# Splitting the branch and gate products of block 1 into quarters of the contraction, between seven parts of the modulation weights

## The reference

```
mod = silu(c) @ w_ada + b_ada                  # w_ada: 2048 x 6144
shift, scale, gate = split(mod, 3)
h = rms_norm(x) * (1 + scale) + shift
xr, gr, qc, kvc, kr, ga = split(h @ w_in)      # widths 1024, 1024, 512, 512, 64, 1024
y_rnn = rg_lru(conv4(xr)) * silu(gr)           # causal conv of width 4, two 64x64 block gates, scan
y_att = mla(rms(qc) @ w_uq, rms(kvc) @ w_ukv, rope(kr)) * silu(ga)    # 8 heads, causal
x = x + gate * (concat(y_rnn, y_att) @ w_out)
```

## Time and profile before

| what | us |
|---|---|
| median of 3 runs (lowest, highest) | 2844.11 (2840.98, 2847.81) |
| the profiled execution's own time | 2841.78 |
| its span, first to last instruction | 2840.0 |
| TensorE busy in the span | 2769.7 (98%) |
| first lora product starts | 56.62 |
| last lora product ends | 201.03 |
| output product of block 1 starts | about 415 |

### The profile page before, as it was taken

The page is one execution under the profiler, slowest core; times in us unless marked ns, Lnnn a source line. Parts: engine busy times, 40 slices in busy tenths (PEclk is TensorE's granted clock), DMA queues, the critical chain, the costliest instruction groups (busy, mean ns, idle before and its releaser), DMA issues.

```text
span 2840.0 us, 43925 instructions
## 1 busy us (share of the span) xinstructions
PE 2769.7 (98%) x15316; PEld 2382.7 (84%) x15316; DVE 1964.4 (69%) x2557; ACT 1191.3 (42%) x1519; POOL 5.7 (0%) x10
## 2 busy tenths in 40 slices
PE   5999999999999999999999999999999999999999
PEld 3778788888878888888888888888888888888888
DVE  5446457666766777756777775687777775677765
ACT  1012434444444444444444443355444444444443
POOL 0000000000000000000000000000000000000000
PEclk9999999999999999999999999999999999999999
DMA  9787556544444666656666566654466666666664
GB/s 328 249 267 210 192 171 193 167 137 156 148 134 155 187 190 185 185 190 187 191 185 186 181 198 190 185 163 128 150 188 183 188 188 191 186 189 185 190 197 146
DMA packets 693729, 526.63 MB, mean 185 GB/s; under 512 B 28877, under 2 KB 674831, under 8 KB 693391
## 3 DMA queue, kind: packets, MB, share of 16 engines
q1 hardware_dynamic: 690448, 521.04, 59.8%
q10 hardware_dynamic: 3199, 4.48, 0.4%
HBM read 523.34 MB, written 2.10 MB: 185 GB/s over the span
## 4 chain that ended last, share of the span: by engine, by line
PE 91%; DVE 4%; issue 2%; ACT 2%; DMA 1%; ACTq 0%; DVEq 0%; SPq 0%
PE acc L623 76%; PE acc L704 3%; PE acc L882 2%; PE acc L688 1%; PE turned L704 1%; DVE wr L1622 1%; PE sums L704 1%; DVE pro_ada L1697 1%; PE mixed L804 1%; PE sums L999 1%; PE sums L631 0%; PE mixed L1004 0%; DMA pro_xrow<-in_x 0%; ACTq L1212 0%; ACT wr L1181 0%
## 5 line engine op out<-in xcount | busy, mean ns | idle before, releaser
L623 PE MATMUL acc<-xs,wr 128*128 128x512 f32 (+1 forms) x7680 | 1365.2, 339 | 1.1 <-DVE wr L1622 1.1
L623 PEld LDWEIGHTS acc<-xs,wr 128*128 128x128 f32 x7680 | 1176.6, 188 | 177.4 <-issue 7.2
L1622 DVE TENSOR_TENSOR wr<-raw,wr 128x1024 fp32r<-128x1024 f32 x832 | 1001.3, 1222 | 360.4 <-ACT wr L1181 348.7
L1181 ACT ACTIVATE wr<-raw 128x1024 fp32r<-128x1024 f32 x832 | 869.6, 1056 | 816.6 <-PE acc L623 809.2
L623 PE MATMUL acc<-ys,wr 128*128 128x512 f32 (+1 forms) x4352 | 770.0, 339 | 6.0 <-DVE ys L1656 5.8
L623 PEld LDWEIGHTS acc<-ys,wr 128*128 128x128 f32 x4352 | 668.8, 189 | 102.6 <-DVE ys L1656 6.4
L623 PE MATMUL acc<-wr,xs 128*128 128x512 f32 (+1 forms) x1024 | 190.1, 344 | 0.0
L623 PEld LDWEIGHTS acc<-wr,xs 128*128 128x128 f32 x1024 | 158.2, 188 | 27.0 <-issue 4.3
L1515 ACT ACTIVATE ffn_cv<-ffn_cv 128x256 f32<-128x256 f32 x88 | 36.8, 419 | 245.5 <-DVE ffn_cv L2177 245.5
L1633 DVE TENSOR_REDUCE ffn_ug<-acc 128x512 f32<-128x1024 f32 x88 | 107.7, 1224 | 42.6 <-PE acc L623 42.6
L1697 DVE SCALAR_TENSOR_TENSOR pro_ada<-aring,small,pro_ada 128x1024 f32<-128x1024 f32 (+1 forms) x80 | 85.6, 1070 | 59.5 <-DMA aring<-in_w_ada 55.3
(11 more groups left out here) (297 smaller groups left out, 1492.2 us busy)
## 6 DMA issues: line engine op xcount, KB each, us to landing
raw<-in_ffn_w_up SPq DMA_DIRECT2D x704, 256.0 KB
raw<-in_ffn_w_down SPq DMA_DIRECT2D x160, 512.0 KB
raw<-in_a_w_qkv SPq DMA_DIRECT2D x96, 512.0 KB
raw<-in_b_w_kv SPq DMA_DIRECT2D x64, 512.0 KB
aring<-in_w_ada SPq DMA_DIRECT2D x48, 512.0 KB, 10.6
w<-in_w_in SPq DMA_DIRECT2D x48, 512.0 KB
raw<-in_w_ada SPq DMA_DIRECT2D x32, 512.0 KB, 5.1
raw<-in_w_out SPq DMA_DIRECT2D x32, 512.0 KB
```

The source lines that it names most:

```text
L623: mm = pe.matmul(*ops, start=first and ops is wide, stop=last and ops is wide)
L1181: f(wr[:, s, :, 0:256], raw[:, s, :].rearrange("p (k n) -> p k n", k=UK), ACT.Copy)\
L1622: tt(wr[:, s, :, 256:512], raw[:, s, :].rearrange("p (k n) -> p k n", k=UK), wr[:, s, :, 0:256], ALU.subtract).then_inc(T.unit_split[s].se ...
```

## The change

- `ADA_PARTS` has seven parts in place of five: tiles 0-1, 2-3, 4-5, 6-7, 8-11, 12-13, 14-15. A load for a part of two tiles is 256 KB in runs of 1 KB; for four tiles 512 KB in runs of 2 KB.
- xr and gr are made in quarters of the contraction. Quarter 0 of all 8 pairs is put aside by ScalarE; quarters 1 and 2 are added to `half` by VectorE (`quarter_out`). Quarter 3 comes after the loras for xr and after U_PAIRS for gr.
- TensorE's order: parts 0 and 1 with lora(0..3); quarter 0, then part 2; lora(4), lora(5), part 3, lora(6), lora(7); quarter 1, then part 4; lora(8..11); quarter 2 with part 5 in it; lora(12), part 6, lora(13..15). SyncE's loads are reordered to match.
- The ring holds variable spans of one area of 8192 columns (1152 for lora, 1024 for the rest).
- The 64 columns of kr are loaded twice, side by side, and multiplied in one matmul of 128 columns.
- x is loaded by SyncE ahead of w_ada, not by ScalarE after the vectors. Its transposes come before those of the vectors and use two PSUM banks in turn.
- The roots' sums of q, kv and kr each stand behind their own unit of xr.
- ScalarE evaluates the recurrence's gates g-1 before it waits for v unit g, not after.
- gr's last quarter stands before ga, with the attention heads starting in it. The recurrent half of the output is gated within the head loop, ahead of the attention half, and the output product takes the contraction tiles from 0 instead of from 8.

```diff
-ADA_PARTS = [(0, 4), (4, 4), (8, 4), (12, 2), (14, 2)]
+ADA_PARTS = [(0, 2), (2, 2), (4, 2), (6, 2), (8, 4), (12, 2), (14, 2)]
-LORA_COLS = 2 * LORA + ROPE
+LORA_COLS = 2 * LORA + 2 * ROPE
+ONE_RING, ONE_SPACE = 8, RING * UK * 512
...
+            sp.dma_start(xrow[:, :, :], t["x"][0]...)          # SyncE, before the positions
...
+            for part in range(2):
+                for r in range(KT):
+                    ada_load(part, r)
+                    if r in (6, 14):
+                        lora_load(2 * part + r // 8)
             for r in range(KT):
                 ada_load(2, r)
+                if r % 2 == 0:
+                    quarter_load(r // 2, 0)
+            lora_load(4)
...
+            for i in range(8):
+                quarter_load(i, 2)
+                for r in range(4 * i, 4 * i + 4):
+                    ada_load(5 + r // KT, r % KT)
...
-                for e in range(2):
-                    mm = pe.matmul(scores[e * ROPE:(e + 1) * ROPE, 0:TOK], wl[:, s, 2 * LORA:LORA_COLS], xm[:, k, :], ...)
+                mm = pe.matmul(scores[:, 0:TOK], w[:, 2 * LORA:LORA_COLS], xm[:, k, :], ...)
...
+            def quarter(q, columns=()):
+                for i in range(8):
+                    n = 8 * q + i
...
+                    if 2 <= n <= 9:
+                        pe.wait_ge(F.half_out.sem, n - 1)
+                    if n > 9:
+                        pe.wait_ge(F.half_added.sem, n - 9)
+                    two_tiles(halves((turned, sums)[i % 2]), xm, q * UK)
+                    if i in columns:
+                        mod_columns(columns[i])
             for part in range(2):
                 mod_columns(part)
+                lora(2 * part)
+                lora(2 * part + 1)
+            quarter(0, {7: 2})
+            lora(4)
+            lora(5)
+            mod_columns(3)
+            lora(6)
+            lora(7)
+            quarter(1, {7: 4})
+            for k in range(8, 12):
                 lora(k)
+            quarter(2, {4: 5})
+            lora(12)
+            mod_columns(6)
+            for k in range(13, KT):
+                lora(k)
...
+            def quarter_out(q, i):                              # VectorE
+                dve.wait_ge(F.w1_used.sem, QUARTER_AT[q] + i + 1)
+                here = half[:, 2 * i:2 * i + 2, :]
+                tt(here, two((turned, sums)[i % 2]), here, ALU.add).then_inc(F.half_added.sem, 1)
...
+            for i in range(8):
+                ada_rows(4, 1 + 2 * i, min(3 + 2 * i, KT))
+                quarter_out(1, i)
             modulated(4)
+            for i in range(8):
+                for r in range(4 * i, 4 * i + 4):
+                    ada_rows(5 + r // KT, r % KT, r % KT + 1)
+                quarter_out(2, i)
+                if i == 5:
+                    modulated(5)
+            modulated(6)
...
+                if what == "v" and g:                           # ScalarE, before the wait for unit n
+                    gates(g - 1)
                 act.wait_ge(F.w1_used.sem, U_AT + n + 1)
...
-            residual_product(from_tile=KT // 2)
+            residual_product()
```

More of the change, by code:

```diff
@@ L644, in _ @@
                 mm.then_inc(F.turned_ready.sem, 1)
[L646 to L650, removed]
-                    for e in range(2):
[L652 to L659, removed]
+            pe.wait_ge(*F.scores_read.next())
             one_units = [0]
@@ L748, in lora_sums @@
[L748 to L751 removed]
+                squares = {"q": sq, "kv": S, "kr": tmp}[what]
+                m = const(C_ONES64) if what == "kr" else ones[:, :]
+                for c in range(1 if what == "kr" else LT):
+                    mm = pe.matmul(mixed[:, 0:TOK], m, squares[c // 2][:, c % 2, :], start=c == 0,
+                                   stop=what == "kr" or c == LT - 1)
@@ L865, in attention @@
                     latent_turn(at // 2 - 1)
-                if at >= 5 and (at - 5) % 4 == 0 and at < 18:
+                if at >= 5 and (at - 5) % 4 == 0:
                     latent_out((at - 5) // 4)
-                if slot == 24:
+                if slot == 3:
                     gate_sums(0)
-                if slot == 41:
+                if slot == 19:
                     gate_sums(1)
             F.mixed_read.n = 2
+            for i in range(4):
+                two_tiles(halves(take(GR_BANK[i])), xm, 3 * UK)
+                attention(i)
             for g in range(4):
@@ L884, in _ @@
                     mm.then_inc(F.w1_used.sem, 1)
-                    attention(22 + 4 * g + u)
-            for i in range(4):
-                two_tiles(halves(take(GR_BANK[i])), xm, KT // 2, 2, after=lambda j: attention(38 + 2 * i + j))
+                    attention(4 + 4 * g + u)
             fresh = {"scores", "turned", "mixed", "sums"}
@@ L967, in after @@
                                 meanwhile(n)
-                        pair(lambda k: ys[:, (k + from_tile) % blocks, :], blocks, before=gated if first and e == 0 else None, after=after)
+                        pair(lambda k: ys[:, k, :], blocks, before=gated if first and e == 0 else None, after=after)
                 per = dict(acc_read=2, **splits(2 * -(-blocks // UK)))
@@ L1213, in _, with root_of @@
                    .then_inc(T.vec_in.sem, 16)
-            act.dma_start(xrow[:, :, :], t["x"][0].rearrange("(m p) d -> p m d", p=P)).then_inc(T.x_in.sem, 16)
+            act.preload_act_table_set(LN_EXP)
+            for g in range(KT // 2):
+                here, ready, read = ((turned, F.turned_ready, F.turned_read), (scores, F.scores_ready, F.scores_read))[g % 2]
+                act.wait_ge(*ready.next())
+                if g >= 2:
+                    act.wait_ge(*F.sums_ready.next())
+                f(flat(sq[g % 2][:, :, :]), here[:, :], ACT.Square).then_inc(F.sq_ready.sem, 1)
+                f(flat(h[:, 2 * g:2 * g + 2, :]), here[:, :], ACT.Copy).then_inc(*read.one())
+            def root_of(bank_sums, n, to, read, ready):
+                f(to, bank_sums, ACT.Ln, scale=1.0 / n, bias=epsc[:, 0:1]).then_inc(*read.one())
+                act.wait_ge(read.sem, read.now())
+                f(to, to, ACT.Exp, scale=-0.5).then_inc(ready.sem, 1)
+            act.wait_ge(*F.sums_ready.next(2))
+            root_of(sums[:, 0:TOK], D, rs[:, 0, :], F.sums_read, F.rs_ready)
             for k in range(PACKS):
```

363 lines of the change are left out of this document (169 added, 194 removed).

## The result

The changed kernel takes 2835.23 us (median of 8 runs, 2833.66 to 2838.92), beside 2843.41 for the kernel before in 8 runs on the same chip (2840.98 to 2847.81). The ratio is 0.9972, 95% interval [0.9961, 0.9983]. It is faster by 8.2 us. I had forecast 7.9 and 2836.2.

A forecast was written before the change was run, and what follows sets the result against it. TensorE, busy 98% of the span and 91% of the chain of waits, was taken as the bound. Terms -10.1 (start and loras), +5.5, -4.5 and +1.2 made -7.9, from 2844.1 to 2836.2 us; range 2826 to 2848.

The forecast's parts named there:

- start, first lora: Before the first lora: early x load and two banks bring lora(0) from 56.62 to 40.0, -16.6 us.
- first to last lora: From lora(0) to the last lora: new waits outweigh the cheaper kr, +6.5 us net, ending at 218.5.
- to the third head_sums and behind it: Between loras and U_PAIRS: TensorE waits 4.5 for ScalarE's square, plus 1.0 for the clock, +5.5 us.
- v units: At the v units: gates run beside the v product, removing three waits of 1.51 each, -4.5 us.
- seam: Before the output product: VectorE and ScalarE need 15.2 us against 14.0 of TensorE work, +1.2.
- The hole: Before part 2's columns: VectorE idle some 19 us, memory idle; TensorE later waits 5.6 for part 3.
- Quarter 2: Third quarter of the xr and gr products: last w_ada parts land near 201, lora(12) at 201.2, not 198.9.
- kr: In each of 16 loras: one full-width kr product takes 0.43 instead of 0.58, 2.4 us gained.
- (a): Rival: smaller holes, VectorE catches up in U_PAIRS and the seam has no wait; 2830.5 us, chance 0.17.
- (b): Rival: holes stay, two more restarts run slow, quarter 2 loses 2 more; 2841.4 us, chance 0.14.
- (c): Rival: halved w_ada loads hold memory back in quarter 2, slower by 4; 2848 us, chance 0.14.
- (d): Rival: ring spans come free late, two quarters wait some 3 us each for weights; 2842 us, chance 0.10.

The follow-up runs named there:

- e4: Changed kernel with x loaded by ScalarE behind its vector loads again, as in the kernel before; 2844.45 us, ratio to the kernel before 1.0005.
- e1: Changed kernel with part 2's columns summed behind the third unit of quarter 0, not the eighth; 2824.81 us, ratio to the kernel before 0.9940.
- e2: Changed kernel with conv(3) in the sixth turn of VectorE's loop over U_PAIRS, not the second; 2829.61 us, ratio to the kernel before 0.9956.
- e5: Changed kernel with kr's 64 columns loaded once and multiplied in two matmuls again; 2838.73 us, ratio to the kernel before 0.9980.
- e3: Changed kernel with ScalarE evaluating gates g-1 behind the copy of v unit g again; 2838.79 us, ratio to the kernel before 0.9982.
- e6: Changed kernel with w_ada's last two parts made one of four tiles, columns behind quarter 2; 2834.02 us, ratio to the kernel before 0.9968.
- e8: e7 with one ready lora (5, 7, 11) kept back behind the columns of parts 3, 4 and 5; 2814.66 us, ratio to the kernel before 0.9896.
- e7: Changed kernel with the edits of e1, e2 and e6 together; 2821.59 us, ratio to the kernel before 0.9923.

## Why the prediction came out right, step by step

The forecast's sum was -7.9 and the measured difference of medians -8.2. The profile allows each term to be checked:

| term | predicted | in the trace |
|---|---|---|
| start, first lora | -16.6 (at 40.0) | -16.6 (at 40.02) |
| first to last lora | +6.5 | +8.1 |
| to the third head_sums and behind it | +5.5 | +7.1 |
| v units | -4.5 | -5.2 |
| seam | +1.2 | +0.7 |
| to the output product | -7.9 | -6.0 |

The terms of the last column make -5.9, and the output product came 6.0 earlier. Behind it another 0.5 went, which makes the 6.5 of the spans. The remaining 1.7 of the 8.2 is scatter of the executions: that of before was 1.6 below its kernel's median, that of the changed kernel on it. So the prediction was right in its mechanism, term by term, but that 8.2 lies so close to 7.9 is luck: in the profiles, where each term can be seen, the sum is 1.9 short of what I said.

*The start* was right in its sum and in its parts: x's first transpose is at 10.36 (load near 10), VectorE normalises from 33.32 (33.2), and lora(0) is at 40.02 (40.0). That it agrees to 0.02 us is luck too, since kernels with this start had their first lora from 38.2 to 40.5. e4 shows that x's load is half of it.

*The hole* was right in place and in mechanism. I had VectorE idle for some 19 us before `modulated(2)`; it is 14.56, and the missing part stands just ahead of it as a wait of 3.76 for a row of part 3. The memory beside it was not idle, as I had said, but moved 147 GB/s. Part 3's columns waited 5.57 (5.6 said), lora(6) started at 113.87 (113.0). e1 takes the cause away and 9.1 us go. I had read the hole at 82 in the kernel before as worth little, which no run tested; the new hole in the same place cost more than the whole change gained.

*Quarter 2* waited 2.94 for its weights (2.3 said).

*The third head_sums* waited 4.17 (4.5 said), and e2 shows that its cause was the one named. *kr* came as said (e5). *The v units* brought 5.2 and not 4.5: I had priced the waits and left out the 0.24 us that the product behind each wait costs more (e3). At *the seam* the wait was 0.71, where I had taken 1.2.

*What I sized wrongly* is one term in both rows of the table that are off: what TensorE runs behind a wait. For lora(8) I had counted none, and its first 16 instructions took 5.38, which is 1.7 more than the 3.69 at full rate. The trace of before had held the same thing, 16 columns (at 78.37) with a short wait behind them, and I had not read it:
```profile
82.62 5.21 PE L688 MATMUL acc<-xm,wl 128*128 128x256 f32 x16 [1.14 <-DVE xm L1715]
```
Behind the 4.17 us wait I had counted 1.0, halfway between two rows; the two sums took 2.07 and the unit behind them 5.55, where the same work took 1.02 and 3.62 at full rate, so 3.0 in all. The window from 257 to 266 shows why: the granted clock is 0.62 there, so part of it ran at 1.2 GHz. These are 1.7 + 2.0 = 3.7 us beyond the sum. The two rows of the table are off by 1.6 each, 3.2: quarter 2 cost 0.6 more, while lora(6)'s slow start (5.27, where I had counted 2.5 more than 3.65) and the shorter wait at `head_sums` gave some 1.2 back.

*The rivals.* (a), smaller holes, is refuted by the waits at 111.01 and at 258.08. (b), holes with two more slow starts and quarter 2 losing 2 more, was half right: the slow starts, lora(8) and the unit behind `head_sums`, came and cost 3.7 beyond the sum where it had 3.2, but quarter 2 lost only 0.6 more than forecast. The v units (0.7), the seam (0.5) and lora(6) (0.9) gave half of it back. (c), the slower case, had quarter 2 waiting over 5 us; it waited 2.94, and e6 shows that to be all that the small loads cost there. (d), a ring that frees spans too late, did not happen: the waits for weights go with the size of w_ada's loads (e6), in an unchanged ring.

## What to carry over

When an engine stands idle beside a fully busy TensorE, follow its list on: what it would have done in that time is what somebody waits for later, and a step moved a few units earlier (e1, one number in the code) can be worth more than the change around it. Where one engine must hand a small result to another and get it back, keep one finished piece of work behind the hand-over (e8). And price a wait of TensorE with what follows it: 1.00 us came to 2.7 at lora(8), 4.17 us to 7.2.

## What the runs showed of the hardware

The slow instructions behind a wait do not go with the length of the wait alone. Over the changed kernel and e1 to e7, a lora stood eight times behind 8 matmuls one column wide (0.95 us) and a wait of 1.00 to 1.07: its first 16 instructions took 3.69 each time. Ten times one stood behind 16 such matmuls (1.84 to 1.95 us) and a wait of 1.00: they took 5.18 to 5.38 in eight of these and 3.69 in two (lora(8) of e3 and of e5), though the matmuls and the wait ahead of it were the same. (lora(6) behind part 3's columns is left out of both counts where these had waited for over 4 us themselves.) In e8 the same 16 matmuls came without a wait, twice, and the lora behind them took 3.70.

Two more places say that the 8 matmuls are no safe side, and that a shorter wait is none either. lora(0) stands behind 8 of them and a wait of 1.48: over the changed kernel and e1 to e8 it took 3.69 in six profiles and 5.38 in three (e4, e6, e7). In the kernel before, a lora behind 8 of them (which had waited 1.48 themselves) and a wait of 1.00 took 5.38, at 190.84. And the output product stands behind 16 one-column matmuls (1.84 us) and a wait of 0.71 to 0.83: over the same nine kernels the granted clock of its first 6 us was 1.00 in four (the changed kernel, e1, e4, e5) and 0.72 to 0.73 in five, with 25 matmuls done in place of 34, some 1.6 us lost. The changed kernel and e7:
```profile
409.02:415.02 6.00, 6.00 (x34) 5.22 (x35) 4.64 (x5) 3.94 (x5) 0.00 (x0) 1.00 0.72 218
391.00:397.00 6.00, 6.00 (x25) 5.20 (x26) 3.64 (x5) 3.92 (x4) 0.00 (x0) 0.72 0.72 230
```
So the changed kernel was spared at the seam, where I had counted no slow start.

The granted clock beside lora(8)'s slow start was 0.73 in the changed kernel (153.77 to 160.00), and 1.2 GHz for a part of it:
```profile
153.77:160.00 6.23, 6.23 (x21) 5.21 (x22) 3.73 (x7) 0.00 (x0) 0.00 (x0) 0.73 1.10 348
```
At waits under 1.6 us the slow start came, in the rows of this section, where one-column matmuls and a wait stood together (behind the 4.17 us at `head_sums` it came without them). Behind 16 such matmuls without a wait (twice in e8) and behind the waits for weights alone (0.40 to 1.59 us, 3.69 to 3.72 for the 16 instructions) it did not. At these lengths one and the same sequence gave both outcomes. That this is part of the 3 to 5 us by which runs of one kernel differ is likely but not shown: the fastest run of the changed kernel (2833.66) had a mean granted clock of 0.994, the slowest (2838.92) of 0.992.
